# Key scores list by list between the queries, the top sixteen taken from the bank, two score tiles in the first program

## What is computed

```python
def peer_ffn(xn, wq, sub_k1, sub_k2, expert_u, expert_v):      # in blocks of 128 tokens
    q = (xt @ wq).reshape(PEER_BLOCK, PEER_HEADS, 2, PEER_HALF)            # 8 heads, 2 halves of 128
    s1 = jnp.einsum("thd,kd->thk", q[:, :, 0], sub_k1)                     # 128 keys for each half
    s2 = jnp.einsum("thd,kd->thk", q[:, :, 1], sub_k2)
    v1, i1 = lax.top_k(s1, PEER_TOPK)                                      # top 16 of 128
    v2, i2 = lax.top_k(s2, PEER_TOPK)
    cand = v1[..., :, None] + v2[..., None, :]                             # 16 x 16 candidates
    top, pos = lax.top_k(cand, PEER_TOPK)
    eidx = jnp.take_along_axis(cidx, pos, axis=-1)                         # 16 of 16384 experts
    g = jax.nn.softmax(top, axis=-1)
    act = jax.nn.gelu(jnp.einsum("td,thkd->thk", xt, expert_u[eidx]))
    return jnp.einsum("thk,thkd->td", act * g, expert_v[eidx])
```

## Time and profile before

| | before |
|---|---|
| median of 3 runs | 1579.94 us (1579.43 to 1580.34) |
| span of the profiled execution | 1581.2 us |
| instructions | 24953 |
| TensorE busy | 1547.1 us, 98% |
| VectorE, ScalarE, GpSimd busy | 1150.4, 620.2, 1076.6 us |
| DMA | 418.37 MB, mean 265 GB/s |
| first program | until 404.1 us |
| score tiles | 398.5 to 1003.5 us |
| value stage | 1004.4 to 1526.9 us |

### The profile page before, as it was taken

The page is one execution under the profiler, slowest core; times in us unless marked ns, Lnnn a source line. Parts: engine busy times, 40 slices in busy tenths (PEclk is TensorE's granted clock), DMA queues, the critical chain, the costliest instruction groups (busy, mean ns, idle before and its releaser), DMA issues.

```text
span 1581.2 us, 24953 instructions
## 1 busy us (share of the span) xinstructions
PE 1547.1 (98%) x8645; PEld 1392.4 (88%) x8645; DVE 1150.4 (73%) x2401; ACT 620.2 (39%) x936; POOL 1076.6 (68%) x566
## 2 busy tenths in 40 slices
PE   7999999999999999999999999999999999999998
PEld 6987887788999999999999999788888888888886
DVE  6868564401869999999999994576767677785746
ACT  3223772211333333456656564333333333333331
POOL 5444313463579888898766767788887878778763
PEclk9999999999999999999999999999999999999999
DMA  5212213321479999899999998999999999999961
GB/s 203 103 56 79 107 54 112 124 101 56 161 252 344 321 314 310 295 326 357 346 345 360 355 335 290 341 367 359 344 370 375 352 355 356 346 343 344 351 222 53
DMA packets 168229, 418.37 MB, mean 265 GB/s; under 512 B 15952, under 2 KB 90576, under 8 KB 163296
## 3 DMA queue, kind: packets, MB, share of 16 engines
...
## 4 chain that ended last, share of the span: by engine, by line
PE 73%; DMA 1%; ACT 0%; DVE 0%; issue 0%; SPq 0%; ACTq 0%; DVEq 0%
PE psum L1589 33%; PE psum L370 10%; PE psum L371 10%; PE psum L374 10%; PE psum L1573 5%; PE psum L226 1%; PE psum L227 1%; PE psum L217 1%; DMA u_raw<-in_u_t 1%; PE psum L257 0%; ACT s_acts L1653 0%; SPq L1414 0%; PE psum L1561 0%; DVE e_gate L2024 0%; DVE e_nT_lo L2011 0%
## 5 line engine op out<-in xcount | busy, mean ns | idle before, releaser
L1489 POOL TENSOR_TENSOR u_lo<-u_raw,u_hi 128x1024 fp32r<-128x1024 f32 x222 | 547.1, 2465 | 189.6 <-ACT u_hi L1648 186.2
L1648 ACT CAST u_hi<-u_raw 128x1024 fp32r<-128x1024 f32 x254 | 265.7, 1048 | 316.2 <-PE psum L1589 230.6
L370 PE MATMUL psum<-hn_hi,u_hi 128*128 128x368 f32 x1024 | 342.5, 334 | 4.0 <-ACT s_acts L1653 2.6
L371 PE MATMUL psum<-hn_lo,u_hi 128*128 128x368 f32 x1024 | 336.7, 329 | 0.0
L1589 PE MATMUL psum<-u_hi,s_whi 128*128 128x512 f32 x768 | 298.0, 389 | 0.9 <-ACT s_acts L1653 0.9
L1589 PE MATMUL psum<-u_hi,s_wlo 128*128 128x512 f32 x768 | 297.9, 389 | 0.0
L1589 PE MATMUL psum<-u_lo,s_whi 128*128 128x512 f32 x768 | 297.9, 389 | 0.0
L370 PEld LDWEIGHTS psum<-hn_hi,u_hi 128*128 128x128 f32 x1024 | 192.9, 188 | 4.5 <-ACT u_hi L1648 2.8
L371 PEld LDWEIGHTS psum<-hn_lo,u_hi 128*128 128x128 f32 x1024 | 193.1, 189 | 0.0
L1522 POOL DMA_INDIRECT s_vrows<-in_v_t,s_v_row x128 | 174.4, 1362 | 26.7 <-issue 24.9
L374 PE MATMUL psum<-hn_hi,u_lo 128*128 128x368 f32 x1024 | 191.4, 329 | 0.0
...
## 6 DMA issues: line engine op xcount, KB each, us to landing
u_raw<-in_u_t SPq DMA_DIRECT2D x128, 512.0 KB, 6.2
u_raw<-in_v_t SPq DMA_DIRECT2D x128, 512.0 KB, 6.3
act_scratch<-s_acts SPq DMA_DIRECT2D x128, 192.0 KB, 4.7
...
```

Of the source, the lines that this page charges most:

```text
L370: pe.matmul(out, hi[:, d * P:(d + 1) * P], dense(hn_hi, d), start=(d == 0), stop=False)
L371: pe.matmul(out, hi[:, d * P:(d + 1) * P], dense(hn_lo, d), start=False, stop=False)
L1489: pool.tensor_tensor(lo[:, s, :], raw[:, s, :], hi[:, s, :].bitcast(F32), ALU.subtract).then_inc(lo_ready[s], 1)
L1648: act.copy(hi[:, s, :], raw[:, s, :]).then_inc(hi_ready[s], 1)
```

## The change

The bank list puts the scores of list f - 1 behind the query product f (`key_scores`: the four token blocks of one list in one bank), and both u tiles 0 and 1 behind the last. VectorE doesn't copy the scores any more: it takes each list's top sixteen straight from the bank into `best` and `besti`, which now lie at the start of the memory of `scores`, with a small `s_cur` for the list with its first eight struck out. TensorE does score tiles 0 and 1 in the first program, ScalarE casts and GpSimd cuts four there (`U_FIRST` 4). The two weight slots change places, so that the slots of tiles 0 and 1 come free first. In the second program the retrievals begin with `best` and `besti`; the first gather is due at tile 10 and not 15; dots are 0, 8, 10 and 10 in the four retrievals and 32 behind them (60 by tile 64), where there were 3 and three times 16 (51).

```diff
--- before.py
+++ after.py
@@ -64,18 +64,19 @@
 C_END = 64
 
 UR = 4
-U_FIRST = 2
+U_FIRST = 4
 H_AT = 6
 GT = 32
 KB = 1024
 STEP_TOK = 8
 LOOP_A = 72
 EXP_AT, TURN_AT = 64, 68
-FIRST_GATHER = 15
+FIRST_GATHER = 10
 KEPT = 2
 DT = T - P
 U_RING, U_AHEAD = 8, 4
-DOTS_1, DOTS_T, DOTS_M, DOTS_J = 3, 16, 12, 12
+DOTS_T, DOTS_M, DOTS_J = (0, 8, 10, 10), 12, 12
+DOTS_FREE = 32
 DOTS_EXP, DOTS_PRE = 4, 9
 XT = 16
 XG = P // XT
@@ -84,7 +85,7 @@
 
 E_AT, Z_AT, Z_EARLY = 8, 12, 2
 
-DOT_AT = (0, 1, 2, 3, 4, 6, 8, 9, 11, 12, 13, 14, 15, 16, 17, 18)
+DOT_AT = (3, 4, 5, 6, 8, 9, 10, 11, 12, 13)
 
 
 def reached(eng, sem, value):
@@ -143,7 +144,7 @@
 
     def __init__(self, sb, new_sem, tag, count, raw=None, hi=None, lo=None, first_in_pieces=False):
         self.count, self.pieces = count, DC // self.PIECE if first_in_pieces else 1
-        ring = lambda name, dtype: [t[:, i, :, :] for t in [sb(f"{tag}_w_{name}", [P, 2, DC, self.WIDTH], dtype)] for i in range(2)]
+        ring = lambda name, dtype: [t[:, 1 - i, :, :] for t in [sb(f"{tag}_w_{name}", [P, 2, DC, self.WIDTH], dtype)] for i in range(2)]
         self.raw = raw or ring("raw", F32)
         self.hi = hi or ring("hi", F32R)
         self.lo = lo or ring("lo", F32R)
@@ -354,11 +355,13 @@
         add(("h", TB + t), "h_ready", TB + t + 1, FROM_FOUR)
     for c in range(DC):
         add(("hnT", c), "hn_ready", c + 1, FROM_FOUR)
-    for f in range(LISTS):
-        add(("pq", f), "qT_ready", f + 1, FROM_FOUR)
-    for i in range(TB * LISTS // 4):
-        add(("ps", i), "scores_ready", i + 1, FROM_FOUR)
-    add(("u", 0), "scores_ready", TB * LISTS // 4, (0,))
+    for f in range(LISTS + 1):
+        if f < LISTS:
+            add(("pq", f), "qT_ready", f + 1, FROM_FOUR)
+        if f:
+            add(("ps", f - 1), "scores_ready", f, FROM_FOUR)
+    for n in range(2):
+        add(("u", n), "scores_ready", LISTS, (n,))
     return out
 
 
@@ -412,7 +415,8 @@
 
     h = shared["h"]
     con, cols = shared["con"], shared["cols"]
-    hn_hi, hn_lo, scores, hn_at = (shared[k] for k in ("hn_hi", "hn_lo", "scores", "hn_at"))
+    hn_hi, hn_lo, hn_at = (shared[k] for k in ("hn_hi", "hn_lo", "hn_at"))
+    best, besti = shared["best"], shared["besti"]
     hn = (hn_hi, hn_lo)
     N_XBC = 6
     N_PLE = N_XBC + XBC_C // 2
@@ -473,6 +477,7 @@
         qkT = at("m_qkT", [P, 2 * DIFF_H, T], 48)
         e = at("e_raw", [P, TB, D], 16)
         pin = at("e_p", [P, TB, PLE], 0)
+        s_cur = at("m_s_cur", [P, TB, NK], 40)
         yd = [at(f"m_yd_{part}", [P, DC // 2, T], 48 + 8 * i, F32R) for i, part in enumerate(("hi", "lo"))]
         y_part = lambda part, d: nT[part][:, d, :] if d < DC // 2 else yd[part][:, d - DC // 2, :]
         ang = sb("m_ang", [P, 5, TB, HD // 2])
@@ -572,7 +577,7 @@
                 weights.load(sp, N_Q + n, io["w_q"][n])
             for n in range(N_Q + LISTS // 2 - 2, N_Q + LISTS // 2):
                 sp.wait_ge(weights.lo_ready[n % 2], weights.cuts(n))
-                for s in (2 * (n % 2), 2 * (n % 2) + 1):
+                for s in (2 * (1 - n % 2), 2 * (1 - n % 2) + 1):
                     sp.dma_start(u_raw[:, s, :], io["u_t"][s]).then_inc(tile_loaded[s], 16)
             sp.wait_ge(sem["h_stored"], 16 * TB)
             sp.wait_ge(sem["row_ready"], 2)
@@ -814,24 +819,28 @@
                 scan_sums(1, t)
 
             turn_blocks(pe, bank, "hnT", sem["hxn_ready"], 1, lambda t, c: xn(t)[:, c * P:(c + 1) * P], ident)
+            def key_scores(f):
+
+                pe.wait_ge(sem["qT_ready"], f + 1)
+                out = bank.take(pe, "ps", f)
+                for t in range(TB):
+                    last = pe.matmul(out[:, t * NK:(t + 1) * NK], qx[:, f, t * P:(t + 1) * P], keys[:, f % 2, :], start=True, stop=True)
+                tile_done(last)
+
             for f in range(LISTS):
                 w = weights.ready(pe, N_Q + f // 2)
                 out = bank.take(pe, "pq", f)
                 sides = (lambda part, d: w[part][:, d, (f % 2) * P:(f % 2 + 1) * P]), (lambda part, d: hn[part][:, d, :])
                 if f == 0:
                     tile_done(moving_product(pe, out, *sides, sem["hn_ready"], sem["hhigh_ready"]))
+                    pe.wait_ge(sem["k_loaded"], 16)
                 else:
                     tile_done(product(pe, out, *sides))
-            pe.wait_ge(sem["k_loaded"], 16)
-            pe.wait_ge(sem["qT_ready"], LISTS)
-            for i in range(TB * LISTS // 4):
-                t, f0 = i // 4, (i % 4) * 4
-                out = bank.take(pe, "ps", i)
-                for j in range(4):
-                    last = pe.matmul(out[:, j * NK:(j + 1) * NK], qx[:, f0 + j, t * P:(t + 1) * P], keys[:, j % 2, :], start=True, stop=True)
-                tile_done(last)
-            pe.wait_ge(hi_ready[0], 1)
-            score_products(pe, bank.take(pe, "u", 0)[:, 0:DS], u_hi[:, 0, :], u_lo[:, 0, :], hn, (lo_ready[0], 1)).then_inc(tile_used[0], 1)
+                    key_scores(f - 1)
+            key_scores(LISTS - 1)
+            for s in range(2):
+                pe.wait_ge(hi_ready[s], 1)
+                score_products(pe, bank.take(pe, "u", s)[:, 0:DS], u_hi[:, s, :], u_lo[:, s, :], hn, (lo_ready[s], 1)).then_inc(tile_used[s], 1)
 
         @block.scalar
         def _(act):
@@ -1000,12 +1009,18 @@
                 src = bank.filled(act, "hnT", c)
                 me.did(act.activation(hn_hi[:, c, :], src, ACT.Copy, scale=col(cols, C_FFN + c)), sem["hhigh_ready"])
             weights.unused(act, N_Q - 1)
+            def round_rows(s):
+                act.wait_ge(tile_loaded[s], 16)
+                act.copy(u_hi[:, s, :], u_raw[:, s, :]).then_inc(hi_ready[s], 1)
+
             for f in range(LISTS):
                 src = bank.filled(act, "pq", f)
                 me.did(act.copy(qx[:, f, :], src), sem["qT_ready"])
-            for s in range(U_FIRST):
-                act.wait_ge(tile_loaded[s], 16)
-                act.copy(u_hi[:, s, :], u_raw[:, s, :]).then_inc(hi_ready[s], 1)
+                if f == LISTS - 2:
+                    for s in range(2):
+                        round_rows(s)
+            for s in range(2, U_FIRST):
+                round_rows(s)
 
         @block.vector
         def _(dve):
@@ -1245,10 +1260,22 @@
             me.did(dve.tensor_tensor(h[:, TB - 1, :], xn(0), gain, ALU.mult), sem["row_ready"])
             dve.wait_ge(sem["pe_tile"], bank.index[("hnT", DC - 1)] + 1)
             me.did(dve.tensor_tensor(xn(TB - 1), xn(TB - 1), gain, ALU.mult), sem["row_ready"])
-            for i in range(TB * LISTS // 4):
-                src = bank.filled(dve, "ps", i)
-                me.did(dve.tensor_copy(scores[:, i // 4, (i % 4) * 4:(i % 4) * 4 + 4, :], src.rearrange("p (l k) -> p l k", k=NK)),
-                       sem["scores_ready"])
+            for f in range(LISTS):
+                src = bank.filled(dve, "ps", f).rearrange("p (t k) -> p t k", k=NK)
+                for t in range(TB):
+                    me.did(dve.max(best[:, t, f, 0:8], src[:, t, :]))
+                me.settle()
+                for t in range(TB):
+                    me.did(dve.max_index(besti[:, t, f, 0:8], best[:, t, f, 0:8], src[:, t, :]))
+                for t in range(TB):
+                    me.did(dve.match_replace(s_cur[:, t, :], best[:, t, f, 0:8], src[:, t, :], LOWEST), sem["scores_ready"] if t == TB - 1 else None)
+                me.settle()
+                for t in range(TB):
+                    me.did(dve.max(best[:, t, f, 8:16], s_cur[:, t, :]))
+                me.settle()
+                for t in range(TB):
+                    me.did(dve.max_index(besti[:, t, f, 8:16], best[:, t, f, 8:16], s_cur[:, t, :]))
+            me.settle()
     new_sem.free()
 
 
@@ -1258,8 +1285,9 @@
 
 
     con, hn_hi, hn_lo, scores, h = (shared[k] for k in ("con", "hn_hi", "hn_lo", "scores", "h"))
+    best, besti = shared["best"], shared["besti"]
     hn_row = h[:, TB - 1, :]
-    OPS = 5 * LISTS + 3 + 2 * len(BLOCKS) + 5 * PH + 2 + 6 + 4
+    OPS = 3 + 2 * len(BLOCKS) + 5 * PH + 2 + 6 + 4
     n_steps = NK
     turns = n_steps // UR
     n_body = DT // (8 * STEP_TOK)
@@ -1318,17 +1346,12 @@
         idi = after_match[:, 2 * PAIRS:4 * PAIRS].rearrange("p (j n) -> p j n", j=2).bitcast(I32)
         expert = psum[:, 2, 3 * PAIRS:4 * PAIRS].bitcast(I32)
         cut = {}
-        at = 0
-        for name, n in (("s_cur", LISTS * NK), ("best", LISTS * TOPK), ("bestf", LISTS * TOPK)):
-            cut[name] = work[:, 1, at:at + n]
-            at += n
+        bestf = work[:, 1, 0:LISTS * TOPK].rearrange("p (l k) -> p l k", l=LISTS)
         for name, bank, at_col, n in (("left", 2, 0, PAIRS), ("leftf", 2, PAIRS, PAIRS), ("cand0", 3, 0, PH * CAND),
                                       ("cand1", 6, 0, PH * CAND), ("cid", 7, 0, PH * CAND), ("posf", 2, 2 * PAIRS, PAIRS)):
             cut[name] = psum[:, bank, at_col:at_col + n]
-        assert at <= NK * GT and PH * FIRST * CAND + 4 * PAIRS <= NK * GT
```

(43 more changed lines are left out.)

## The result

The changed kernel takes 1584.03 us in the median (20 executions, 1581.78 to 1585.01), the kernel before, run on the same chip at the same time, 1580.88 (20, 1579.43 to 1585.54). The ratio is 1.0017, with a 95% interval of 1.0011 to 1.0023: slower, by 1.7 to 3.6 us. The forecast was 1579.3, 0.6 us faster, with a range of 1575.5 to 1583.8: the time lies just above the range, and the change went the other way. The profiled execution has a span of 1581.9 us and a time of its own of 1583.63.

What follows compares the result with a forecast made beforehand. TensorE, busy 98% of the span, was taken as the bound, so only its waits could move. Terms -0.9 + 1.1 + 0 + 1.9 + 1.7 + 0 - 4.4 = -0.6 us gave 1579.3 us, range 1575.5 to 1583.8.

Steps and rivals of the forecast that it cites:

- Part 1: Key scores between the queries: -0.9 us of idle before the scores, +1.1 us for 14 returns at 0.08 each.
- Part 2: VectorE's top sixteen from the bank: 5.1 us a list against TensorE's 6.4, finishing under the two score tiles; 0 us.
- Rival 5: VectorE falls behind in the bank at over 6.4 us a list, barrier 9 us late: about 1588 us, chance 0.03.
- Part 3: Two score tiles ahead of the barrier: tile 2 waits there for ScalarE's table load and tile 0's Gelu, +1.9 us.
- Part 4: The clock falls behind the 3.3 us gap at the barrier, slowing TensorE: +1.7 us.
- Part 5: Retrieval and gathers in the second program: earlier first gather costs 0 us, earlier last gathers give -4.4 us.
- late end: Before the values: nine gathers leave the last score tiles, tile 126 lands in time, wait and slow tile go, -4.4 us.
- Rival 2: Tile 126's transfer stays late behind the value weights in its own queue: +3.8 us, 1583.7 us, chance 0.14.
- early end: First gather at tile 10: GpSimd waits 1 to 2 us near pair 26, keeping 2.7 us before TensorE feels it; 0 us.
- rival 4: Gathers block GpSimd, TensorE waits for low parts around tiles 30 to 34: 3 to 5 us more, 1583.5, chance 0.05.
- differences over unchanged: Base of the sum: differences from the profiled span of 1581.2 us applied unchanged to the unprofiled median of 1579.94 us.

Runs made afterwards that it cites:

- e_copy: Kernel before with only the key scores moved between the queries, VectorE just copying each bank to SBUF: 1582.51 us, ratio 1.0008.
- e_mid: Changed kernel with each list's scores in the middle of the next query product, list 15's inside score tile 0: 1581.79 us, ratio 1.0009.
- e_table: Changed kernel plus a one-column Gelu ending ScalarE's first program, so the table loads ahead of the barrier: 1581.37 us, ratio 1.0005.
- e_late: Changed kernel with 23 and not 32 dots behind the retrievals, so 51 pairs are gathered by tile 64: 1587.25 us, ratio 1.0033.
- a_again: The changed kernel, unchanged, in another profiled execution: 1584.16 us, ratio 1.0022.
- e_dots: Changed kernel with the second retrieval's eight dots at later pauses of VectorE: 1583.46 us, ratio 1.0013.
- e_pool: Changed kernel with the first gather due at tile 12 and not 10: 1593.01 us, ratio 1.0078.
- b_again: The kernel before, unchanged, in another profiled execution: 1582.26 us, ratio 1.0008.

## Why the prediction was wrong

- **Part 1** held: 1.1 us for the returns was 0.7 (e_copy). The 0.08 had been read from the first tile behind the barrier, which follows a gap and not key scores.
- **Part 2 is the step that failed.** The list time of 5.1 us was right (5.2), and VectorE kept up with TensorE list by list. The sentence "After the last score bank it has 5 us left, under the two score tiles (8.1 us)" was wrong. Part 1 had put list 14's scores right in front of list 15's, so both banks were full within a microsecond, and VectorE had two lists left: 10.4 us against 0.9 us of scores and 8.1 of tiles. After the last score bank (397.49) it had 9.7 us left and not 5. The prediction's own part 1 says that the two lists come together. I had read the cover from the list rate, and the last two lists don't come at that rate. Instead of "VectorE's last operation some 3 us before TensorE's last product" it came 1.46 us after it. Cost: 1.46 us by the profile, 1.70 by e_mid. Rival 5 asked only for a list time over 6.4 us, and missed this.
- **The Trainium skill's rule against part 2.** Here four MAX8 on the bank take 0.89 us and four on SBUF 0.88 (the rows at 396.82 and 400.00). The surcharge is 0.01 us for four. The Trainium skill (VectorE: DVE Perf Modes, errata table) has 62 cycles more for each; the trace doesn't agree.
- **Part 3** was right in size: table and Gelu 1.91 us of 1.9, the table 1.28 of it (e_table). The Gelu began 0.01 us behind the load. The drain that the Trainium skill adds (ScalarE: Activation LUTs, "What ACT_TABLE_LOAD costs") is not seen here either.
- **Part 4** was right in kind and too small: the clock fell, one fall in two profiles of a 5 us gap (the changed kernel, e_late) and two in three others (a_again, e_dots, e_pool), at 1.7 us each, so 2.7 in the mean and not 1.7. The longer gap may be the reason: 3.29 us had none (e_mid, one profile, and an unusually fast one), 3.71 had one (e_table). That is argued, not shown.
- **Part 5, late end**, was right in its mechanism: 2.56 us of wait and 1.7 of clock are gone from the profile, 4.3 for the 4.4. With the nine gathers back the changed kernel pays 1.90 + 1.7 (e_late). Rival 2 fell. How much of it an ordinary execution wins is less sure, since the fall of the clock was not in e_copy. **Its early end** was mis-sized: the 2.7 us of margin counted was less than none, and TensorE waited 0.68 us at tile 33, between tiles 25 and 40, where the prediction had named such a wait as a sign that it was wrong. That is rival 4's mechanism at its place, at a smaller price. The hand count hadn't weighed how strongly VectorE's wait for the first row moves everything behind it (e_pool).
- **The base.** I took the median of three executions, 1579.94; over 20 it is 1580.88, 0.9 more. And "differences over unchanged" was a step without support: a profiled span lies 1.7 to 1.8 us under the same execution's own time (1580.4 and 1582.22 in b_again, 1581.9 and 1583.63 for the changed kernel), so the span of 1581.2 belongs to an execution of about 1583.0, an estimate, 2 us over the kernel's median.

The sum: 1.7 for the gap (4.99 and not 3.3), 1.0 for the second fall, 0.7 at tile 33 and 0.9 of base, less 0.4 for the returns, is 3.9 of the 4.7 us by which the median missed the forecast. The remaining 0.8 stays open. The stretches differ by 1.4 us in the first profile (2.5 with a_again's) and the medians by 3.15. One candidate is the base again: both profiles of the kernel before had the late fall of the clock, and both took long, the first by the 2 us above, the second with 1582.22 beside a median of 1581.20 over 29 (though not beside that of its own twelve, 1582.26). If the ordinary execution has it more seldom, as e_copy's didn't, part 5 wins less in the median than the 4.3 read from the profile. The profiles of one execution each can't show how often it falls.

That the time came out beside rivals 2 and 4 (1583.7 and 1583.5) is luck: the first mechanism wasn't there, and the second cost 0.7 us.
